# Fifteen expert pairs scattered to device memory, and one combined by token products, in place of fourteen and two

## The reference

```python
h = h + token_mixer(rms_norm(h, ln1_g[l]), ...)
h = h + hier_moe(rms_norm(h, ln2_g[l]), w_group[l], ..., w1[l], w3[l], w2[l])
...
# hier_moe: each token picks one of 4 groups and 2 of its 8 experts (32 experts in all)
def expert_block(args):
    xb, e = args
    hdn = jax.nn.silu(xb @ w1[e]) * (xb @ w3[e])
    return hdn @ w2[e]
...
out = jnp.zeros((T + 1, D), ys.dtype).at[slot_tok].add(ys * slot_w[:, None])[:T]
```

## Time and profile before

| | us |
|---|---|
| median of 3 runs (1455.4 to 1460.04) | 1455.99 |
| span of the profiled execution | 1454.1 |
| TensorE busy in it | 1386.9 |
| VectorE busy | 453.7 |
| ScalarE busy | 475.4 |
| GpSimd busy | 484.8 |

### The profile page before, as it was taken

How to read it: one execution, slowest core, us unless ns; L and a number is a source line. 1 busy time by engine, 2 the same in 40 slices (tenths; PEclk the granted TensorE clock), 3 DMA queues, 4 the chain that set the end, 5 groups by cost and what they waited for, 6 DMA issues and landing times.

```text
span 1454.1 us, 19158 instructions
## 1 busy us (share of the span) xinstructions
PE 1386.9 (95%) x7602; PEld 965.1 (66%) x7602; DVE 453.7 (31%) x1080; ACT 475.4 (33%) x839; POOL 484.8 (33%) x240
## 2 busy tenths in 40 slices
PE   7999999999999999988999999999999999998886
PEld 6889877788888633333488988777888885333333
DVE  3332644410233412112333335443113243211114
ACT  4522476632332111111253326765223321111112
POOL 3633433456660111111144443335565401111111
PEclk9999999999999999999999999999999999999999
DMA  7522222224377999999962213222243789999996
GB/s 266 180 88 87 73 73 73 73 89 150 109 233 303 357 414 419 419 420 416 388 240 88 88 59 109 73 73 73 74 165 121 260 324 374 420 420 420 420 413 268
DMA packets 136467, 331.24 MB, mean 228 GB/s; under 512 B 16629, under 2 KB 98629, under 8 KB 113848
## 3 DMA queue, kind: packets, MB, share of 16 engines
q1 hardware_dynamic: 127736, 314.29, 57.6%
q0 software_dynamic: 8640, 15.69, 2.9%
HBM read 312.17 MB, written 33.55 MB: 238 GB/s over the span
## 4 chain that ended last, share of the span: by engine, by line
PE 77%; DMA 15%; DVE 2%; SPq 2%; ACT 1%; issue 1%; POOL 0%; DVEq 0%; POOLq 0%; ACTq 0%
PE ps L583 18%; PE ps L585 17%; PE ps L584 17%; DMA w<-in_w 13%; PE ps L998 12%; SPq L476 1%; PE ps L799 1%; PE ps L779 1%; PE ps L787 1%; PE ps L735 1%; DMA yb<-y_dram 1%; PE ps L896 1%; PE ps L945 1%; PE ps L990 1%; DMA raw<-in_w_in 1%
## 5 line engine op out<-in xcount | busy, mean ns | idle before, releaser
L583 PE MATMUL ps<-uH,ringH 128*128 128x512 f32 x704 | 275.5, 391 | 0.0
L584 PE MATMUL ps<-uL,ringH 128*128 128x512 f32 x704 | 274.0, 389 | 0.0
L585 PE MATMUL ps<-uH,ringL 128*128 128x512 f32 x704 | 274.0, 389 | 0.0
L998 PE MATMUL ps<-w,xT 128*64 128x512 f32 x1024 | 229.9, 600 | 10.1 <-DMA w<-in_w 9.3
L998 PEld LDWEIGHTS ps<-w,xT 128*64 128x64 f32 x1024 | 77.5, 138 | 154.7 <-issue 149.2
L998 PE MATMUL ps<-w,hT 128*64 128x512 f32 x512 | 125.5, 635 | 34.2 <-DMA w<-in_w 22.8
L1438 POOL TENSOR_TENSOR ringL<-raw,ringH 128x2048 fp32r<-128x2048 f32 x28 | 128.7, 4603 | 79.2 <-ACT ringH L1147 79.2
L583 PEld LDWEIGHTS ps<-uH,ringH 128*128 128x128 f32 x704 | 132.2, 188 | 28.2 <-issue 0.7
L585 PEld LDWEIGHTS ps<-uH,ringL 128*128 128x128 f32 x704 | 132.1, 188 | 27.7
L584 PEld LDWEIGHTS ps<-uL,ringH 128*128 128x128 f32 x704 | 132.2, 188 | 27.2
L1482 POOL TENSOR_TENSOR ringL<-raw,ringH 128x2048 fp32r<-128x2048 f32 x32 | 147.0, 4594 | 5.1 <-ACT ringH L1296 5.1
(11 more groups left out here) (281 smaller groups left out, 2101.2 us busy)
## 6 DMA issues: line engine op xcount, KB each, us to landing
w<-in_w SPq DMA_DIRECT2D x176, 1024.0 KB, 15.3
raw<-in_w_in SPq DMA_DIRECT2D x54, 1024.0 KB, 5.2
w<-in_w SPq DMA_DIRECT2D x32, 512.0 KB, 16.6
raw<-in_w_out SPq DMA_DIRECT2D x8, 1024.0 KB, 5.3
yb<-y_dram SPq DMA_DIRECT2D x8, 1024.0 KB, 15.7
braw<-in_w_branch SPq DMA_DIRECT2D x24, 256.0 KB, 4.5
h_dram<-hs SPq DMA_DIRECT2D x2, 2048.0 KB, 11.5
y_dram<-attT SPq DMA_DIRECT2D x8, 512.0 KB, 8.9
```

The lines of the kernel that those rows point to most:

```text
L583: mm(o, h, rh, start=first, stop=False)
L584: mm(o, h, rl_, start=False, stop=False)
L585: return mm(o, l, rh, start=False, stop=last)
L998: ins = mm(o[r], lhs[:, r], rhs[x], start=first, stop=last, skip_group_check=True)
```

## The change

`NS` becomes 15. Pair 14 is now treated as the pairs before it: two DVE instructions into `yy` and a scatter by POOL. Its `tok_of`, its `yH` and `yL`, and its half of all token products fall away; `token_rows` loses the argument that named the pair. The wait in front of the reading of `y_dram` is now for fifteen scatters instead of fourteen; the wait for pair 14's down product stays (its count was written as `NS + 1` and is now `NS`, both 15).

```diff
-SLOTS, W2_SLOTS, NS = 4, 5, NP - 2
+SLOTS, W2_SLOTS, NS = 4, 5, NP - 1
...
             hold(sp, y_stored.h, y_stored.at(lay, 16 * NS))
-            hold(sp, down_filled.h, down_filled.at(lay, NS + 1))
+            hold(sp, down_filled.h, down_filled.at(lay, NS))
...
-                token_rows(5, 0, True, False)
-                token_rows(5, 1, False, False)
+                token_rows(5, False)
...
                 for x in (6, 7):
-                    token_rows(x, 0, True, False)
-                    token_rows(x, 1, False, False)
+                    token_rows(x, False)
                     other_rows(lay - 1, x)
...
-                hold(pe, tokens_ready.h, tokens_ready.at(lay, 2))
-                for x in (2, 3):
-                    token_rows(x, 0, True, False)
+                hold(pe, tokens_ready.h, tokens_ready.at(lay, 1))
                 for x in range(2 * NT if lay + 1 == L else 5):
                     if x < 2:
-                        hold(pe, last_low.h, last_low.at(lay, x + 2))
-                    elif x > 3:
-                        token_rows(x, 0, True, False)
+                        hold(pe, last_low.h, last_low.at(lay, x + 1))
...
-                else:
-                    hold(pe, last_low.h, last_low.at(lay, 1))
-                    hold(pe, tokens_ready.h, tokens_ready.at(lay, 1))
-                    for x in range(2):
-                        token_rows(x, 0, True, False)
                 pe.wait_ge(hidden_ready.h, hidden_ready.at(lay, p + 1))
...
-                if p == NS:
-                    act.wait_ge(down_filled.h, down_filled.at(lay, p + 1))
-                    fn(yH[0][:], ps[:, A[0] * 512:A[0] * 512 + 1024], ACT.Copy).then_inc(last_high.h, 1)
-                    return
...
-                if p == NS:
-                    dve.wait_ge(down_filled.h, down_filled.at(lay, p + 1))
-                    slot_tokens(tok_of[0], slice(p, p + 1)).then_inc(tokens_ready.h, 1)
-                    dve.wait_ge(last_high.h, last_high.at(lay, 1))
-                    v.tensor_tensor(yL[0][:], ps[:, A[0] * 512:A[0] * 512 + 1024], yH[0][:].bitcast(f32), ALU.subtract).then_inc(last_low.h, 1)
-                    return
-                slot_tokens(tok_of[1], slice(p, p + 1)).then_inc(tokens_ready.h, 1)
+                slot_tokens(tok_of, slice(p, p + 1)).then_inc(tokens_ready.h, 1)
```

More of the change, by code:

```diff
@@ L157, in trunk @@
     yy = sb("yy", [P, D], f32, R_T1 + 28 * KB)
-    yH = [sb(f"yH{x}", [P, D], f32r, R_O + 4 * x * KB) for x in range(2)]
-    yL = [sb(f"yL{x}", [P, D], f32r, off) for x, off in enumerate((R_T1 + 4 * KB, R_O + 28 * KB))]
-    tok_of = [sb(f"tok_of{x}", [P, S], f32r, R_T1 + 2 * x * KB) for x in range(2)]
+    yH = sb("yH", [P, D], f32r, R_O + 4 * KB)
+    yL = sb("yL", [P, D], f32r, R_O + 28 * KB)
+    tok_of = sb("tok_of", [P, S], f32r, R_T1 + 2 * KB)
     tok_w = sb("tok_w", [P, S], f32r, R_O + 20 * KB)
```

20 lines of the change are left out of this document (10 added, 10 removed).

## The result

The changed kernel takes 1463.77 us (median of 6 runs, 1461.6 to 1465.35) against 1456.36 us (6 runs, 1455.4 to 1460.04). The ratio is 1.004 with a 95% interval of 1.0029 to 1.005. That is slower by 0.4%, where I had forecast no change (1455.4 us, range 1453 to 1459.5). The time lies 4.3 us above the range.

A forecast was written before the change was run, and what follows sets the result against it. Each expert stage was taken to end when its last weights arrive. The span of 1454.1 us, less 1.25 in layer 0, plus 0.7 in layer 1, gave 1453.55; with 1.9 for the median, 1455.4 us, range 1453 to 1459.5.

The forecast's parts named there:

- The chain of layer 1: Layer 1's end: pair 14's down product, `yy`, scatter, SP's issue, `yb[1]`, POOL; sixteen products saved there worth 0.
- The products x = 6 and 7 of layer 0: Four token products on the path ahead of tile 2's transposes in layer 0; removing them gains 0.94 us.
- The first four products: Layer 0, x = 2 and 3, ahead of x = 0: 0.94 us on the path, 0.3 taken as gain.
- A late issue alone is hidden in layer 0: Layer 0's later `yb[0]` issue costs nothing, since the next layer's first unit stands ahead on the line.
- The idle microsecond under the hidden rows is harmless: Layer 0, x = 0 and 1: removal worth 0; PE's idling harmless as long as its clock stays full.
- this was the pure transfer. Now the line is nearly empty.: Layer 1: issue 9.35 us later, but mostly stood in line behind w2, so `yb[1]` comes only 0.7 us later.
- The 1.6 us of fixed time: Fixed part of a `yb` read's landing, from a 256 KB transfer taking 2.2 us, 0.6 of them bytes.
- My upper bound for this term: Most that layer 1 could lose: 3.9 us, with 2.1 for the slowest scatter and 1.1 for slow 1 MB loads.
- the scatter's bytes, 0.63 us: Layer 0: the scatter's 0.26 MB join the line, so `yb[0]` lands between 718.0 and 718.65 us.
- Nothing else becomes late: Layer 0: w2 of pair 15 landed at 712.65 us, wanted at 713.42; units 1 to 3 not late either.
- the rival in which the scatter goes ahead of weights: Scatter's 0.63 us falls before the last weights, moving all of layer 0's end: 1456.0 us; chance 0.18.
- That the reads keep their 15.7 us from the issue: Rival: behind a fresh scatter `yb` lands 9.3 us later in both layers, 1473.7 us; chance 0.10.

The follow-up runs named there:

- the repetition: The changed kernel run once more, unchanged, on the same chip as the other follow-ups: median 1464.84 us, ratio 1.0059.
- the wait alone: The kernel before, with the reads of `y_dram` also waiting for the transposes of pair 15's hidden rows, no fifteenth scatter: 1463.13 us, ratio 1.0035.
- the cover out: The kernel before, without pair 14's four token products for x = 0 and 1, so that PE idles there: 1458.06 us, ratio 1.0004.
- the scatter alone: The changed kernel, its fifteenth scatter going to a tensor nobody reads, the reads waiting for fourteen only: 1460.27 us, ratio 1.0017.
- mended: The changed kernel with two idle products before pair 15's down product, the gain behind `yb[1]` and DVE's register loads ahead of pair 15: 1462.33 us, ratio 1.0041.
- the improved old kernel: The kernel before, with the gain issued behind `yb[1]` and DVE's register loads ahead of pair 15: 1456.84 us, ratio 0.9992.
- the filler: The changed kernel with two idle products on PE where it waits for pair 15's hidden rows: 1462.31 us, ratio 1.0022.
- the wait with the later gain: The kernel before with the later wait ahead of the reads, no fifteenth scatter, and the gain issued behind `yb[1]`: 1461.11 us, ratio 1.002.

## Why the prediction was wrong

**Right:**
- *The chain of layer 1.* It runs over D, `yy`, the scatter, SP, `yb[1]` and POOL as described, and 32 products on PE are worth nothing there.
- *The products x = 6 and 7 of layer 0.* They were forecast at 0.94 us and gave 0.92, in both traces of the changed kernel.
- *The first four products, by luck.* Forecast at 0.3 us, they gave 0.4 in the profiled execution, where the slow down product gave `yb[0]` the time to land and DVE's register loads (1.45 us behind the `yL` of the earlier trace rows, which I had missed) set the pace. In the repetition they gave nothing: that stretch became 0.2 us longer, since PE waited for `yb[0]`.
- *A late issue alone is hidden in layer 0.* With the wait alone it costs 0.2 us. The scatter's traffic isn't hidden: with it `yb[0]` is 1.1 us late there (forecast 0 to 0.65), whenever it was issued.
- *The idle microsecond under the hidden rows is harmless.* So it is by itself, in the one trace of the kernel with the cover out. The condition that I put to it ("as long as its clock stays full") is the point where it failed in one execution of the changed kernel, in which w2 was late as well; which of the two let the clock fall is not shown. Its premise, a clock that is full throughout, was a misreading of the strip.

**Wrong, the step that decides: "this was the pure transfer. Now the line is nearly empty."** From 2.5 us between the landings of w2 and `yb[0]` I concluded that the reads only stood in line, and that the line turned to them when w2 had landed. But w2's landing is the last engine's. The windows show that 2.1 MB of the 4.72 MB had been moved by then, 5 us of a full line. The counts show the same: twelve of the sixteen parts of `yb[0]` had landed 1.4 us before w2's last one. A landing-to-landing distance tells the pace of the slowest engine; it doesn't tell how much work the others have already done. The term came out at +4.6 us for `yb[1]` where I had +0.7:
- the scatter, 8.0 us for 7.0, and 2.38 for 2.29 up to its issue, and 0.15 until SP issues: together 10.57 for the 9.4 that the text names, +1.2;
- the reads, 10.69 us for 7.9, +2.8. Of it 0.7 is the start, 0.6 the gain's slow stretch and 1.5 the one part of `yb[1]` that comes behind the other fifteen. The 1.6 us of fixed time were too short, 2.3 measured (4.74 to 4.80 us for layer 1's `yb[0]` in all six traces with the late issue, 2.5 of them its bytes). They were read from a store of 256 KB, behind which nothing stands, and such a transfer can't show the lag of one engine either.

My upper bound for this term, 3.9 us, was built from the slowest scatter and the 5.2 us of a single load. It was closer, and still short of 4.6. The scatter wasn't the slowest one (8.04 us for the 9.1 that the bound allows); the bound failed because it set the fixed time of one load against a burst of three.

**Wrong, too: the scatter's bytes, 0.63 us, and "Nothing else becomes late".** W2 of pair 15 had 0.77 us to spare. In the changed kernel it came 1.2 us (layer 0) and 1.0 us (layer 1) later, nearly twice the time of the bytes, and PE's product began 0.5 us later in layer 0. This is the direction of the rival in which the scatter goes ahead of weights, to which I had given 0.18. The rule of the Trainium skill, DMA: Bandwidth & Descriptors, "Queues, rings and completion order", that I quoted with it (an engine serves its queues in turn) gets the direction right in all five traces with a fifteenth scatter. My price of 0.63 us was too low, since these traces show 0.7 to 1.2.

**The rivals.** That the reads keep their 15.7 us from the issue didn't happen: they took 10.69. Yet its mechanism, the wait for the fifteenth scatter, is the right one; the truth lies between it and the forecast, and I gave this middle a chance only as a spread within 0.10. The estimate by the Trainium skill, DMA: Bandwidth & Descriptors, "Anatomy of one DMA — SWDGE (gpsimd) path" (about 2.0 us and the bytes at 436 GB/s), gives 8.0 us for `yb[1]`; it is stated for a single transfer that POOL issues, and these are three that SP issues. The trace has 10.69, and the measurement decides.

**The whole sum.** Of the 9.5 us between the predicted span (1453.55) and the profiled one (1463.1), layer 1's end is 4.0, layer 0's end 2.0 and 3.5 lie elsewhere, where the clock fell in untouched code; that the clock made all of the 3.5 isn't shown. In the repetition of the same kernel layer 0's part was 1.1 and not 2.0. By the medians the wait alone costs 5.9 us and the scatter alone 3.0, and both together 7.4, so they don't add up.

**Open:** whether the changed kernel makes the stretches at 1.2 GHz in the small products more frequent. They stood in the traces of after (both layers), after again (layer 0), mended (layer 0) and the improved old kernel (layer 1), and not in those of before, the filler, the cover out, the wait alone, the scatter alone and the wait with the later gain. Ten single executions don't settle it. A lower clock goes along with the spread among runs of one kernel: in the first group a run of before took 1456.6 us with a mean granted clock of 0.986, and another 1462.29 us with 0.981. I didn't try to remove them. Open too is why one of the sixteen parts of `yb[1]` comes 1.4 to 1.5 us late in layer 1 in five of the six traces with the late issue and not in the mended one; the trace doesn't name the engine.

## What to carry to other kernels

Before moving the issue of a transfer to a later point because "it only stands in line", multiply GB/s by time in windows between the landings: what was moved ahead of the previous landing is what the early issue buys. Work saved on an engine that waits at the end of a stage is worth nothing, while a dependence put in front of the last reads (product, scatter, reads of the same rows) has its whole latency on the path. Before forecasting from one trace of a kernel whose runs spread by 5 us, look for places where the granted clock can fall, since a difference of that size may be in code that the change doesn't touch.

## What the runs showed of the hardware

- **Landings trail bytes.** In a burst of reads of 1 MB the second landed when 0.9 MB of the ones behind it had also been moved (2.2 us at 420 GB/s); fifteen of its sixteen parts had landed 1.5 us before. On the line that had been full all along it was 1.7 of the 2.1 MB behind it, and the parts of one transfer (w2 before) landed over 5.7 us.
- **A burst on an empty line starts slowly:** 86 GB/s on average in the first two microseconds behind the issue (the wait alone). Layer 1's first megabyte landed 4.74 to 4.80 us behind its issue in all six traces with the late issue.
- **A broadcast load is slow.** One row of 4 KB for 128 partitions (512 KB written) brings the line from 420 to some 290 GB/s for two microseconds (279 to 295 in after and the wait alone); moving it away gave `yb[1]` 2.07 us, where its bytes are 1.25.
- **An indirect scatter of 0.26 MB** landed 6.7 to 7.7 us behind its issue for pair 13 and 7.9 to 8.4 us for pair 14 in the kernels that wait for it, and 8.3 and 8.8 us in the two layers where the reads were issued before it. It delayed the weights of the queue beside it by 0.7 to 1.2 us.
- **TensorE's granted clock fell without an idle time that explains it.** In the small products (64 columns) PE is busy all through the windows at 142 to 149 us, and the clock is 1.00 in the trace of before and 0.58 in that of after. Pair 15's down product, behind the same waits of 1.1 and 1.0 us, ran at 1.2 GHz in one execution of the changed kernel (5.23 us) and at 2.4 GHz in another (3.65 us). The Trainium skill, TensorE: Matmul & The Clock Gate, Part 1, states that the chip's observation of the engine's activity runs freely and isn't tied to the kernel's start; this would fit an outcome that differs between executions, and no run here shows it directly.
- **Loads of registers can count.** DVE's reads of a range out of memory take up to 1.45 us between two of its instructions. They are on the chain in one trace (after, layer 0), where nothing else came later; in that of before the chain runs over PE's sums instead, and moving the loads away changed nothing (28.72 us for 28.71). The timeline shows such a time only as a gap ended by "issue".
